# Neighbourhood attention over windows of 32 grid columns, and the router's chain done tile by tile with the first expert's table first

## What is computed

```python
h = rms_norm(x, norm_g)
dq, dk, dv, nq, nk, nv, gates = split(h @ w_in)        # 6 x 512 columns, 2 x 1024 gate columns
y_diff = diff_attention(...)                           # 4 heads, every key of the group
y_na   = neighborhood_attention(nq, nk, nv, rpb)       # 8 heads of 64, tokens as rows of a grid 64 wide
merged = sigmoid(g_d) * (y_diff @ w_br_diff) + sigmoid(g_n) * (y_na @ w_br_na)
x = x + merged @ w_out

t = rms_norm(x, norm2_g)                               # per group: n tokens, 16 experts
aff = softmax(t @ w_router)
gate, idx = top_k(aff.T, 2 * n // 16)                  # 32 prompt and 64 sample tokens an expert
ye = (silu(t[idx] @ w_gate) * (t[idx] @ w_up)) @ w_down * gate
y = x + scatter_add(ye, idx)
```

## Time and profile before

| | us |
|---|---|
| median of 3 runs | 2284.01 (2282.57 to 2286.64) |
| the profiled execution | 2284.7 |
| its span, first to last instruction | 2282.8 |
| TensorE busy | 2187.5 (96%) |
| VectorE busy | 1602.6 (70%) |
| ScalarE busy | 1392.4 (61%) |
| GpSimd busy | 161.4 (7%) |
| moved | 618.75 MB, 271 GB/s |

### The profile page before, as it was taken

How to read it: one execution, slowest core, us unless ns; L and a number is a source line. 1 busy time by engine, 2 the same in 40 slices (tenths; PEclk the granted TensorE clock), 3 DMA queues, 4 the chain that set the end, 5 groups by cost and what they waited for, 6 DMA issues and landing times.

```text
span 2282.8 us, 30905 instructions
## 1 busy us (share of the span) xinstructions
PE 2187.5 (96%) x12116; PEld 1897.2 (83%) x12116; DVE 1602.6 (70%) x1267; ACT 1392.4 (61%) x1115; POOL 161.4 (7%) x116
## 2 busy tenths in 40 slices
PE   6999999999992999999999999999999999999997
PEld 5867878888781999988999889998889988899886
DVE  5366354223417788888888888888888888888885
ACT  5365345222312677777777777777776777767774
POOL 2102200000010000100101001010010100101010
PEclk9999999999995999999999999999999999999999
DMA  5111110112423799999999999999999999999995
GB/s 224 62 48 35 56 62 25 56 56 90 180 86 115 283 366 376 373 368 380 364 375 371 364 375 367 375 374 367 378 361 378 370 371 377 358 382 366 374 371 186
DMA packets 68927, 618.75 MB, mean 271 GB/s; under 512 B 8112, under 2 KB 8496, under 8 KB 16144
## 3 DMA queue, kind: packets, MB, share of 16 engines
q1 hardware_dynamic: 61632, 592.47, 67.1%
q0 software_dynamic: 6816, 25.30, 3.9%
q10 hardware_dynamic: 432, 0.34, 0.0%
HBM read 605.50 MB, written 12.58 MB: 271 GB/s over the span
## 4 chain that ended last, share of the span: by engine, by line
PE 86%; DVE 5%; ACT 4%; issue 3%; DMA 1%; POOL 0%; ACTq 0%; DVEq 0%; POOLq 0%
PE PS L412 26%; PE PS L414 26%; PE PS L413 26%; PE PS L488 2%; DVE x_w_low L947 2%; PE PS L500 2%; ACT x_w_high L875 2%; PE PS L694 1%; PE PS L512 1%; PE PS L421 1%; DVE hidden L1250 1%; PE PS L600 1%; DMA gathered<-t_dram,idxi 0%; ACT s L785 0%; ACT w_high L713 0%
## 5 line engine op out<-in xcount | busy, mean ns | idle before, releaser
L947 DVE TENSOR_TENSOR x_w_low<-x_w_raw,x_w_high 128x2816 fp32r<-128x2816 f32 (+2 forms) x384 | 1182.6, 3090 | 246.7 <-ACT x_w_high L875 245.4
L875 ACT ACTIVATE x_w_high<-x_w_raw 128x2816 fp32r<-128x2816 f32 (+2 forms) x384 | 978.8, 2557 | 249.0 <-PE PS L414 213.8
L412 PE MATMUL PS<-x_w_high,xT_high 128*96 128x352 f32 x2048 | 667.1, 326 | 1.4 <-DVE xT_low L947 1.4
L414 PE MATMUL PS<-x_w_high,xT_low 128*96 128x352 f32 x2048 | 660.2, 322 | 0.0
L413 PE MATMUL PS<-x_w_low,xT_high 128*96 128x352 f32 x2048 | 657.5, 321 | 0.0
L412 PEld LDWEIGHTS PS<-x_w_high,xT_high 128*96 128x96 f32 x2048 | 330.1, 161 | 6.6 <-issue 4.3
L413 PEld LDWEIGHTS PS<-x_w_low,xT_high 128*96 128x96 f32 x2048 | 332.3, 162 | 2.4
L414 PEld LDWEIGHTS PS<-x_w_high,xT_low 128*96 128x96 f32 x2048 | 331.5, 162 | 1.5
L412 PE MATMUL PS<-x_w_high,hidden_high 128*96 128x512 f32 x704 | 280.0, 398 | 2.3
L413 PE MATMUL PS<-x_w_low,hidden_high 128*96 128x512 f32 x704 | 278.1, 395 | 0.0
L414 PE MATMUL PS<-x_w_high,hidden_low 128*96 128x512 f32 x704 | 277.8, 395 | 0.0
(11 more groups left out here) (146 smaller groups left out, 1819.0 us busy)
## 6 DMA issues: line engine op xcount, KB each, us to landing
x_w_raw<-in_w_expert_gate SPq DMA_DIRECT2D x128, 1408.0 KB, 8.2
x_w_raw<-in_w_expert_up SPq DMA_DIRECT2D x128, 1408.0 KB, 8.6
x_w_raw<-in_w_expert_down SPq DMA_DIRECT2D x96, 1536.0 KB, 8.2
x_w_raw<-in_w_expert_down SPq DMA_DIRECT2D x32, 1024.0 KB, 6.8
w_raw<-in_w_in SPq DMA_DIRECT2D x20, 1024.0 KB, 4.8
x<-in_x_sample SPq DMA_DIRECT2D x8, 512.0 KB, 14.2
w_raw<-in_w_out SPq DMA_DIRECT2D x4, 1024.0 KB, 5.0
bias<-in_bias_na POOLq DMA_DIRECT2D x8, 448.0 KB, 3.5
```

Source lines behind the costliest of these rows:

```text
L412: mm(out, sh, mh, start=first, stop=False)
L414: return mm(out, sl, mh, start=False, stop=last)
L875: a_(xh[:, w % SPLITS, 0:n], xraw[:, w % RAWS, 0:n], ACT.Copy).then_inc(x_high, 1)
L947: return v.tensor_tensor(out, src, high.bitcast(F32), ALU.subtract)
```

## The change

Attention: the queries of the sample are laid out by blocks of 16 grid columns (8 rows x 16 columns make a tile of 128). A sample item has the 256 keys of 8 rows x 32 columns, which start at column 0, 8, 24 or 32, read as a strided window of the keys. For the values products the sample's values are stored to memory and loaded as eight windows of 128 tokens. All prompt items come first, then all sample items. The bias tables are eight of 128 x 384 for the prompt and eight of 128 x 1024 for the sample, still in two buffers. The outputs are put back in token order when they are copied after their transposes.

Router: the output products use two banks, in turn. The residual sum itself is transposed; the norm's gain goes into the router's weights and the reciprocal root into the softmax, so that the normalised tile is only stored. Softmax, transpose of the affinities and copy are done for each tile, between the output products; the prompt's rounds, ranks, one-hots and table as well. The splitting into parts goes from VectorE to GpSimd. After the last tile come the sample's eight rounds and ranks, then the first expert's one-hot and table alone, after which the first gather is issued, and then the other experts' tables, for which the expert loop waits. The low parts of the first two units are made by GpSimd, ahead of the first gather in its queue; that of the third by VectorE after the token parts.

The core of the diff:

```diff
-        def items(heads):
-            return [(h, qt, t0, nt) for h in range(heads) for (t0, nt) in GROUPS for qt in range(nt)]
+        ATT = {"diff": [(h, qt, t0, nt) for h in range(4) for (t0, nt) in GROUPS for qt in range(nt)],
+               "na": [(h, qt, t0, 2) for (t0, nt) in GROUPS for h in range(8) for qt in range(nt)]}
...
+        def out_bank(t, c):
+            return OUT_ORDER.index((t, c)) % 2
...
+                if kind == "gate_d0":
+                    for t in range(2, NT):
+                        sp.wait_ge(S("pn", "pused"), 2 * NT + t + 1)
+                        sp.dma_start(v_dram[(t - 2) * P:(t - 1) * P, :], vv[:, t, :]).then_inc(s_vst, 16)
+                    sp.wait_ge(s_vst, 64)
+                    grid = v_dram.rearrange("(r c) n -> r c n", c=GW)
+                    for j, c0 in enumerate(WINDOWS):
+                        for half in range(2):
+                            sp.dma_start(vw[j // 2][:, j % 2, half, :], grid[4 * half:4 * half + 4, c0:c0 + 32, :]
+                                         ).then_inc(s_vw, 16)
...
-                pool.dma_start(bias[:, b, :], bias_diff[nh] if nh < 4 else bias_na[nh - 4]).then_inc(s_b[b], 16)
+                    pool.wait_ge(S(BIAS[nh - 2][0], "biased"), bias_first(nh - 2) + BIAS[nh - 2][2])
+                pool.dma_start(BIAS[nh][4], BIAS[nh][3]).then_inc(s_b[b], 16)
...
+            for t in range(3):
+                normed(t)
+            parts(R_p, R3_p, 0, 2)
+            for t in range(3, NT):
+                normed(t)
+            parts(R, R3, 2, 4)
+            pool.wait_ge(x_split, RAWS)
+            for w in range(2):
+                n = unit_width(w)
+                pool.wait_ge(x_high, w + 1)
+                nc.gpsimd.tensor_tensor(xl[:, w, 0:n], xraw[:, w, 0:n], xh[:, w, 0:n].bitcast(F32), ALU.subtract
+                                        ).then_inc(x_split, 1)
...
+                            if br == "na" and t0 == 2:
+                                keys = kT[r][:, c, SP_:N].rearrange("p (r c) -> p r c", c=GW)[
+                                    :, :, WINDOWS[qt]:WINDOWS[qt] + 32]
...
+            def out_product(t, c, u, ks=range(4)):
+                n = OUT_ORDER.index((t, c))
+                bank = out_bank(t, c)
+                if u == 0:
+                    pe.wait_ge(*((S("g", "mul"), 3 * NT + bank + 1) if n < 2 else (S("o", "added"), n - 1)))
...
+            router_logits(4)
+            out_product(5, 1, 0)
+            transpose_x(5, (0,))
+            pe.wait_ge(S("rt", "table_prompt"), 1)
+            transpose_aff(4)
+            out_product(5, 1, 1, range(2))
+            router_logits(5, range(4))
+            out_product(5, 1, 1, range(2, 4))
+            transpose_x(5, (1,))
+            router_logits(5, range(4, KD))
+            transpose_aff(5)
...
+            split_units(UNITS)
+            v.tensor_tensor(wrt_v, wrt_v, g2.unsqueeze(2).to_broadcast((P, KD, E)), ALU.mult).then_inc(S("rt", "weights"), 1)
...
+            for r in range(CS // 8):
+                top_round(r == 0, SP_, N, work)
+                if r == 0:
+                    dve.sem_inc(x_split, 1)
+            ranks(work, selT, cumT, SS)
+            dve.wait_ge(S("rt", "rkT"), 2)
+            link(v.tensor_copy(rk, PS[:, 6, 0:4 * E].rearrange("p (t e) -> p t e", t=4)))
+            one_hot(G0, rk[:, :, 0], CS).then_inc(S("rt", "G_first"), 1)
+            dve.wait_ge(S("rt", "table_prompt"), 1)
+            dve.wait_ge(S("rt", "first_slots"), 1)
+            link(table(0, CS, 7, 0, 1))
+            v.tensor_copy(idxi[:, 0:2], idxf[:, 0:2]).then_inc(S("rt", "tables"), 1)
+            for t in range(4):
+                one_hot(G[:, t], rk[:, t, :], CS).then_inc(S("rt", "G"), 1)
+            dve.wait_ge(S("rt", "slots"), 1)
+            link(table(0, CS, 3, 1, E))
...
```

More of the change, by code:

```diff
@@ new lines, in _ @@
+            for t, c in OUT_ORDER[:4]:
+                out(t, c)
+            transpose_x(0)
+            out(2, 0)
+            router_logits(0)
+            transpose_x(1)
+            out(2, 1)
+            router_logits(1)
+            transpose_aff(0)
+            out(3, 0)
+            transpose_x(2)
+            transpose_aff(1)
+            out(3, 1)
+            router_logits(2)
+            out(4, 0)
+            transpose_x(3)
+            transpose_aff(2)
+            transpose_rank(7, cumT_p, 2, 1)
@@ new lines, in _ @@
+            out(4, 1)
+            router_logits(3)
+            out_product(5, 0, 0)
+            transpose_x(4)
+            pe.wait_ge(S("rt", "rk"), 1)
+            transpose_aff(3)
+            pe.wait_ge(S("rt", "parts"), 1)
+            pe.wait_ge(S("rt", "G_prompt"), 1)
+            pe.wait_ge(S("rt", "copied"), 3)
+            for t in range(2):
+                for e in range(E):
+                    i = mm(PS[CS:CAP, 6, 6 * e:6 * e + 6], G_p[:, t, e, :], R3_p[:, t, e].rearrange("p m c -> p (m c)"),
+                           start=(t == 0 and e == 0), stop=t == 1, skip_group_check=True)
@@ new lines, in keep_aff, with top_round, ranks @@
+            def keep_aff(t):
+                dve.wait_ge(S("rt", "affT"), t + 1)
+                v.tensor_copy(affT[:, t * P:(t + 1) * P], PS[0:E, 6 + t % 2, 0:P]).then_inc(S("rt", "copied"), 1)
+            def top_round(first, lo, hi, out):
+                link(v.max(m8, affT[:, lo:hi] if first else out))
+                link(v.match_replace(out, m8, affT[:, lo:hi] if first else out, -1.0))
+            def ranks(out, sel, cum, w):
+                link(v.tensor_scalar(sel, out, 0.0, None, ALU.is_lt))
+                link(v.tensor_tensor_scan(cum, one.to_broadcast((E, w)), sel, 0.0, ALU.mult, ALU.add))
+                v.tensor_tensor(cum, cum, sel, ALU.mult).then_inc(S("rt", "rank"), 1)
@@ new lines, in _ @@
+            add_x(0, 0)
+            add_x(1, 0)
+            add_x(0, 1)
+            mean_x(0)
+            norm_x(0)
+            add_x(1, 1)
+            mean_x(1)
+            norm_x(1)
+            add_x(2, 0)
+            softmax(0)
+            add_x(2, 1)
+            mean_x(2)
+            norm_x(2)
+            softmax(1)
+            add_x(3, 0)
+            keep_aff(0)
+            keep_aff(1)
+            dve.wait_ge(S("rt", "copied"), 2)
+            for r in range(CP // 8):
+                top_round(r == 0, 0, SP_, work_p)
@@ new lines, in _ @@
+            add_x(3, 1)
+            mean_x(3)
+            norm_x(3)
+            ranks(work_p, selT_p, cumT_p, SP_)
+            softmax(2)
+            add_x(4, 0)
+            keep_aff(2)
+            dve.wait_ge(S("rt", "rkT"), 1)
+            v.tensor_copy(rk_p, PS[:, 7, 0:2 * E].rearrange("p (t e) -> p t e", t=2)).then_inc(S("rt", "rk"), 1)
+            dve.wait_ge(S("rt", "rk"), 1)
+            for t in range(2):
+                i = one_hot(G_p[:, t], rk_p[:, t, :], CP)
+            i.then_inc(S("rt", "G_prompt"), 1)
```

445 lines of the change are left out of this document (257 added, 188 removed).

## The result

The changed kernel took 2252.11 us (median of four runs, 2249.87 to 2254.89) against 2285.07 for the kernel before: a ratio of 0.9857, 95% interval 0.984 to 0.9874. That is 33 us faster; 43 were forecast (2241 us), and the range (2230 to 2257) held it. The profiled execution took 2251.67 us, its span 2249.9.

The account below looks back on a forecast made before the run. TensorE was taken to bound the expert stage, a fixed block to be started earlier, and attention, the router's tail being one chain. Attention -27 and output and router -16 make -43 from 2284.0: 2241 us, range 2230 to 2257.

Parts of the forecast that it names:

- the rival of late tables: Attention paced by its tables or values: all bias loads take 6.5 us, 15 us back, 2256 us; chance 0.12.
- The rival that hand-offs set an item: Attention: hand-offs, not columns, set an item; at 1.3 us an item 12 us are lost, 2253 us; chance 0.08.
- the 4 + 4 us given back: Attention: 4 us lost to prompt heads' bias loads over two buffers, 4 us to sample-value windows competing with the first loads.
- the 35 us of the items: Attention: 48 items of 1.04 us cost TensorE 50 us, where eight heads took 85.4: 35 less.
- -35 - 2 + 8 + 2: Attention's sum: items -35, last values products -2, bias loads and windows +4 each, hand-offs +2: -27, range -18 to -34.
- 3.8 + 2: Output stage: 3.8 us of tile work moved ahead of the last product, 2 us of added transposes and prompt matmuls.
- the 1.7 us for half clock: Output stage: half clock after TensorE's idle gap of about 3.5 us was counted as 1.7 us more.
- the 2 us of softmax waits: Output stage: TensorE waits for the softmax of tiles 2 and 3, queued on VectorE; 2 us, estimated.
- Output stage: TensorE's output products: the last one ends 13 us later, from 3.8 + 2 + 3.5 + 1.7 + 2, on top of 76.39.
- Tail: Last output product to first expert product: links sum to 34.9 us against 63.91, -29, with a 6.5 us first gather.
- the rival of the two engines that block each other: Router tail: VectorE's compare, scan and product wait for GpSimd's second subtraction; 2244 to 2249 us, chance 0.3.
- GpSimd slow by 10 us or more: Router tail: beyond 7.7 us, each us of a GpSimd subtraction costs two; 2250 at 12 us; chance 0.1 of over 10.

Follow-up runs that it names:

- early_no_windows: The changed kernel with six prompt bias tables loaded during the projection and the sample values' round trip left out (output differs): 2238.22 us, 0.9793.
- tables_early: The changed kernel with the last six prompt bias tables given places of their own and loaded during the projection: 2249.35 us, 0.9849.
- one_sub: The changed kernel with GpSimd making only the first unit's low parts and VectorE the second's: 2248.29 us, 0.9846.
- onehot_psum: The changed kernel with the four one-hots of the other experts reading the ranks in PSUM: 2249.05 us, 0.9843.
- early_unit_first: early_two_queues with the first branch unit's weights loaded ahead of the round trip and the next unit's held until the windows landed: 2240.3 us, 0.981.
- early_two_queues: tables_early with four of the eight window loads issued by GpSimd instead of SP: 2244.11 us, 0.9813.
- no_windows: The changed kernel without storing and reloading the sample's values; its products take the first two value tiles (output differs): 2242.19 us, 0.9818.
- spread_windows: The changed kernel with each window half's keys column by column, so loads read 32 x 4 rows instead of 4 x 32: 2255.94 us, 0.9878.

## Why the prediction was right, and where it was off

**The sum.** The time lies inside the range, but not for the forecast's reasons alone. Attention fell 11 us short of its 27 and missed its own range; the output stage and the tail together took 2.6 us less than summed (121.7 against 89.4 + 34.9), and the range was wide. That the total fell inside is partly luck: at 2252 it lies nearer to the rival of late tables (2256, chance 0.12) than to the forecast's 2241.

**The expert stage** as a fixed block: 1542.7 against 1541.35. Right, within its scatter.

**Items.** 1.04 us forecast, 1.05 measured; ScalarE stays under TensorE. Strided keys in runs of 32 cost nothing (0.43), as taken. The rival that hand-offs set an item is refuted: in the sample part TensorE is busy for 27.38 of 27.60 us.

**The step that failed: the 4 + 4 us given back for the prompt heads' bias loads and for their contention with the windows.** Attention was to gain 27 us, 18 at least; it gained 15.7. From the first logits to the last it is 69.3 us in the changed kernel (302.27 to 371.60) and 54.0 in `early_no_windows` (303.88 to 357.92): tables and windows cost 15.3 us there, 13.9 by the medians, not 8. Two numbers of that step were wrong. For the competition of the windows with the tables it took 4 us, with a doubling of the first three loads as the most (7 to 10); VectorE's five waits for prompt tables sum to 16.2 us. And the windows were expected within 25 us of the attention's start; in `tables_early` they landed 32 us after the store, some 35 after the start. In the changed kernel that costs nothing more, because its first values product with a window comes only at 343.6, behind the late tables. The cause is shown from both sides: without the round trip the tables land in 2.6 to 4.3 us, and with its loads spread the windows land in 3.0 to 6.2. The rival "paced by its tables or values" came true in part: the prompt heads waited, the sample heads 3.1 us in all.

**A second step was mis-sized: the 35 us of the items.** Eight heads of 10.67 us are 85.4, more than the stage's own 83.10, and 48 items of 1.04 us leave out the start, in which TensorE waits 3.9 us in `early_no_windows` until the first item has come through. The gain without any late load is 83.1 - 54.0 = 29. So the forecast's -35 - 2 + 8 + 2 is -29.1 + 15.3, about 0.9 for the clock in the projection, and the rest, 2.8 us of gain, in the last products and the hand-over to the gates.

**Output stage.** 89.4 forecast (76.39 + 13), 85.0 measured. The third product does wait for the first add, which sits behind the last split as forecast: TensorE stops for 2.15 us instead of 3.5 (busy for 1.85 of these 4.00), and the granted clock stays at 1.00:

```profile
596.00:600.00 4.00, 1.85 (x8) 1.19 (x8) 3.13 (x5) 0.00 (x0) 0.00 (x0) 1.00 1.00 422
```

So the 1.7 us for half clock did not come, and the 2 us of softmax waits are not to be found: the gap is all of the stage's idle time (82.83 of 85.00 us busy). The work that was moved and added is 82.83 - 76.39 = 6.4 us against 3.8 + 2. It can't be counted on that no half clock comes: in eight of the twelve kernels here that use two banks, the traces have 0.50 to 0.64 in the 4 us after this gap (last section).

**Tail.** 34.9 forecast, 36.6 measured (670.52 to 707.16). Two terms were off, both upwards: compare, scan and product 4.3 us instead of 2.6, the gather 7.67 instead of 6.5; against that, the softmax link was about 1 us shorter (674.7 to 675.9). GpSimd's subtraction was taken at about VectorE's 3.1 us; it is 6.12, which hits the forecast's estimate of 6.2 from the Trainium skill (GPSIMD Engine Reference, § 3.1), and it was hidden, up to the compare. There the rival of the two engines that block each other came true, just below its price of 3 to 8 us: its own rule gives 2 x (6.12 - 5.0) = 2.2 us for the measured subtraction, and the compare lost 1.9 (2.33 against 0.41 in `one_sub`). The rounds, from 678.29 on beside the subtractions, keep their 1.49 us, and only the compare waits. What the rival did not have is the other direction: the one-hots held the gather, which cost the path 3.3 us more (18.4 against 15.1 in `onehot_psum`) and is why 6.5 was too little. The second gather of the kernel before, which the forecast took as the one beside an idle VectorE, in fact ran its 0.95 us beside 1.1 us of VectorE work with one input in PSUM. The trace agrees with the Trainium skill, SBUF — State Buffer, § Who interferes with whom, in two points: VectorE instructions with two SBUF inputs against a GpSimd that reads, here the one-hots against the gather, which reads its indices; and the compare, a `tensor_scalar` from SBUF to SBUF, an operation that it counts among those that can take both ports. It differs in one: the section infers that a two-input `tensor_tensor` does not hold up the making of a transfer's descriptors, and here the gather's execution took 4.43 us beside such instructions. GpSimd slow by 10 us or more: refuted.

## What to carry to other kernels

When a change makes the computing shorter, ask of each load beside it how long it takes on the queue it will share, not how long it took alone: here some 14 us went there, and removing the first wait alone brought 3 because the second stood right behind it. Look at the DMA share while someone waits: a low share with a late load can mean that the transfer is on few engines, and then another order of its dimensions is worth a run (here 0.26, and landing in 3.0 to 6.2 us with the other order); but the order that suits the load may be wrong for TensorE's reads (0.87 against 0.43 us). And work moved to GpSimd can hold VectorE (the compare, 2.33 against 0.41 us), as VectorE can hold GpSimd (the gather, 4.43 against 1.02 us); leaving one operand in PSUM freed the gather.

## What the runs showed that was not expected

- With window loads of 256 KB from 4 x 32 rows of 2 KB under way, the mean DMA share stood at 0.26 (102 GB/s) for several us, and such a load took up to 16.2 us to land in `early_unit_first` and 19.1 in `early_two_queues`; from 32 x 4 rows it landed in 3.0 to 6.2 us. Loads queued behind the first kind came late too: a table took 20.6 us (`early_two_queues`), a weight unit 19.2 in the changed kernel instead of 4.8, its median.
- One issue of such a load on SP lasted up to 5.8 us in the changed kernel and 7.5 in `tables_early`, with several under way; 0.6 us when they are spread.
- A logit product of 256 keys takes 0.43 us with the keys in runs of 32 and 0.87 with single keys 64 columns apart. The Trainium skill, SBUF — State Buffer, § Door 1, says that SBUF has lines of 16 bytes, four fp32 values, and that an access that crosses to a new line pays a penalty. That fits; that it is the cause no run shows, and the doubling is this trace's.
- GpSimd's indirect gather executed in 0.95 us at its shortest, in 1.02 beside VectorE's one-hots with one SBUF input (`onehot_psum`), and in 4.43 beside the same one-hots with two.
- After TensorE's gap in the output stage the granted clock, over the next 4 us, was 1.00 behind gaps of 1.78 (`one_sub`), 1.95 (`tables_early`), 2.15 (the changed kernel) and 2.42 us (`no_windows`), and 0.50 to 0.64 behind gaps of 2.60 to 3.36 us in seven other kernels. But it was 0.63 behind 2.27 us in `spread_windows`, and 1.00 behind the gap of 3.03 us that the kernel before has at 304.10, so the length of the gap alone does not decide; no run here says what does.
